# Sampled attention: scores in two products with the low rows added by VectorE, and part of the hi/lo splits moved to GpSimd

## The reference, cut to what matters

```python
def sample_attn(q, k, v, lam, k_past, v_past, rel_bias):
    s_past = diff_logits(q, q_pos, k_past, jnp.arange(past), rel_bias)
    s_new = diff_logits(q, q_pos, k, q_pos, rel_bias)
    w = diff_weights(jnp.concatenate([s_past, s_new], axis=-1), lam)   # softmax 0 - lam * softmax 1
    return (jnp.einsum('bhqk,bkhe->bqhe', w[..., :past], v_past)
            + jnp.einsum('bhqk,bkhe->bqhe', w[..., past:], v))
```

## Time and the profile before

| | |
|---|---|
| median of the runs | 2069.2 us |
| profiled execution | 2068.8 us, of which the span is 2066.9 us |
| TensorE matmul busy over the span | 2020.3 us (98%) |
| weight loads / VectorE / ScalarE / GpSimd busy | 1880.8 / 1386.9 / 991.8 / 12.4 us |
| sampled turns (first keys turned to last scores) | 843.5 to about 1073.6 us |
| output projection behind them | up to about 1206 us |

### The profile page before, as it was taken

One profiled execution on the slowest core, in us unless ns is written; L12 is line 12 of the kernel. 1 busy time (PEld: TensorE's weight loads), 2 busy tenths in 40 slices (PEclk: granted clock), 3 DMA queues, 4 the chain that ended last, 5 costly groups with the idle time before them and its releaser, 6 DMA issues. The chain is left out here.

```text
span 2066.9 us, 36364 instructions
## 1 busy us (share of the span) xinstructions
PE 2020.3 (98%) x12096; PEld 1880.8 (91%) x12096; DVE 1386.9 (67%) x3022; ACT 991.8 (48%) x1824; POOL 12.4 (1%) x42
## 2 busy tenths in 40 slices
PE   7999999999999999899999999999999999999998
PEld 6999999999999999888987899999999898989896
DVE  6766676767676766688885467575757574847476
ACT  5757575757575747677774333231313131413133
POOL 0000000000000000000000000000000000000000
PEclk9999999999999999999999999999999999999999
DMA  6411111112111112787782121111202020202012
GB/s 201 138 57 53 56 52 56 58 54 58 49 58 50 58 51 86 293 287 271 284 279 89 58 81 52 36 58 32 62 22 72 22 72 22 62 22 70 12 52 98
DMA packets 167421, 183.01 MB, mean 89 GB/s; under 512 B 11077, under 2 KB 139621, under 8 KB 167317
## 3 DMA queue, kind: packets, MB, share of 16 engines
q1 hardware_dynamic: 166105, 180.98, 27.0%
q10 hardware_dynamic: 1212, 0.81, 0.1%
HBM read 162.56 MB, written 24.46 MB: 90 GB/s over the span
## 5 line engine op out<-in xcount | busy, mean ns | idle before, releaser
L1247 PE MATMUL ps<-h_hi,w_hi 128*128 128x384 f32 (+1 forms) x1152 | 386.5, 336 | 10.2 <-DVE v_lo L1170 6.8
L1247 PE MATMUL ps<-h_hi,w_lo 128*128 128x384 f32 (+1 forms) x1152 | 376.6, 327 | 0.0
L1247 PE MATMUL ps<-h_lo,w_hi 128*128 128x384 f32 (+1 forms) x1152 | 376.4, 327 | 0.0
L2333 PE MATMUL ps<-h_hi,f_w_hi 128*128 128x320 f32 (+1 forms) x1136 | 370.7, 326 | 0.8 <-PEq L1532 0.8
L2333 PE MATMUL ps<-h_hi,f_w_lo 128*128 128x320 f32 (+1 forms) x1136 | 370.4, 326 | 0.0
L2333 PE MATMUL ps<-h_lo,f_w_hi 128*128 128x320 f32 (+1 forms) x1136 | 370.2, 326 | 0.0
L2412 ACT ACTIVATE yc<-ps,f_prm 128x384 f32<-128x384 f32 x144 | 93.5, 654 | 553.8 <-PE ps L2333 391.0
L2313 PE MATMUL ps<-d_hi,act 128*128 128x512 f32 x816 | 257.1, 390 | 1.6 <-DVE d_lo L2516 1.6
L1247 PEld LDWEIGHTS ps<-h_hi,w_hi 128*128 128x128 f32 x1152 | 217.4, 189 | 13.5 <-DVE v_lo L1170 7.2
L1247 PEld LDWEIGHTS ps<-h_lo,w_hi 128*128 128x128 f32 x1152 | 217.0, 188 | 0.6
L1247 PEld LDWEIGHTS ps<-h_hi,w_lo 128*128 128x128 f32 x1152 | 216.7, 188 | 0.0
(11 more groups left out here) (308 smaller groups left out, 3585.3 us busy)
## 6 DMA issues: line engine op xcount, KB each, us to landing
k<-in_cache_k SPq DMA_DIRECT2D x64, 512.0 KB, 5.9
v_raw<-in_cache_v SPq DMA_DIRECT2D x64, 512.0 KB, 4.6
w_raw<-in_w_in SPq DMA_DIRECT2D x48, 512.0 KB, 4.0
f_raw<-in_w_up SPq DMA_DIRECT2D x48, 512.0 KB, 4.0
f_raw<-in_w_down SPq DMA_DIRECT2D x24, 512.0 KB, 3.5
bias<-bias_tiles_dram SPq DMA_DIRECT2D x8, 576.0 KB, 3.7
merged_dram<-mg SPq DMA_DIRECT2D x8, 544.0 KB, 2.7
ow_raw<-in_w_out SPq DMA_DIRECT2D x8, 512.0 KB, 6.4
```

The costliest lines, as they stand in the source:

```text
L1247: last_ = pe.matmul(bank(s)[:, 0:n], w[:, W_SLOT[g], k, :], x[:, k, off:off + n], start=(k == 0 and i == 0), stop=(k == KT - 1 and i == 2))
L2333: l_ = pe.matmul(ps[:, e % 6, 0:n], w[:, p, k, :], x[:, k, off:off + n], start=(k == 0 and i == 0), stop=(k == KT - 1 and i == 2))
```

## The change

The query operand becomes one tile `qd`. For heads 0 to 3 its columns 0 to 63 hold the high parts and 64 to 127 the low parts; for heads 4 to 7 it is the other way round. Two products per chunk (by `kt_hi` and by `kt_lo`) then give the high rows and the low rows of four heads. After heads 0 to 3, and again after heads 4 to 7, ScalarE copies the 64 low rows out of PSUM to `slo` (`low_rows`), and VectorE adds them to the 64 high rows into `P` (`sum_rows`). TensorE's scores of head 4, and of the next turn's head 0, wait for that sum. Bias and maximum are then taken from `P` in SBUF.

The new keys and new values are split once for all sequences (`kn`, `vn`); GpSimd copies the 8 new keys of a head next to the turned ones (`new_key`) and lays the new weights into their own columns (`new_weights`), so that the new values take two matmuls of 128 rows. GpSimd also makes the low parts of value pages 1, 3, 5 and 7, and of output weight rows 0 to 3 in the last turn. The weights are turned before the scores of head 2 in place of after them. Page 2 is applied ahead of the scores of head 4, and later pages mostly one per head. In ScalarE's list `copy_o2` stands ahead of the exponential, and keys stand ahead of the split of the weights.

```diff
-SPLIT_AT = {2: (0,), 3: (1,), 4: (2, 3), 5: (4, 5), 6: (6,), 7: (7,)}
-PV_AT = {4: (0, 1), 5: (2, 3), 6: (4, 5), 7: (6, NPAGES), 8: ()}
+HH = H // 2
+SPLIT_AT = {2: (0, 1), 3: (2,), 4: (3,), 5: (4, 5), 6: (6,), 7: (7,)}
+PV_EARLY = {5: (2,)}
+PV_AT = {4: (0, 1), 5: (3,), 6: (4,), 7: (5,), 8: (6, NPAGES)}
...
+OUT_LOW = [x for x in OUT_SPLITS if x[0] == "m" or x[1] >= 4]
+POOL_LAST = [x for h in range(H + 1)
+             for x in [("v", n) for n in SPLIT_AT.get(h, ()) if n in POOL_PAGES]
+             + [x for x in OUT_AT.get(h, ()) if x not in OUT_LOW]]
...
+    def q_hi_of(part, m, h0):
+        return strips(part, 144 * h0 + DEC_T * m)
+    def q_lo_of(part, m, h0):
+        return strips(part, 144 * h0 + DEC_T * m + (NS if h0 < HH else -NS))
+    def half_rows(s):
+        lo = slice(NS, 128) if s == 0 else slice(0, NS)
+        hi = slice(0, NS) if s == 0 else slice(NS, 128)
+        return hi, lo
...
+            def new_key(b, h):
+                if at_start(b) and h == 0:
+                    pool.wait_ge(new_lo, 1)
+                if not (at_start(b) and h < 2):
+                    pool.wait_ge(qkh_done, 8 * b + h - 1)
+                    pool.sem_inc(settled, 1)
+                pool.tensor_copy(kt[:, :, h % 2, PAST:NKEYS], kn[:, :, h, bass.ds(DEC_T * b, DEC_T)])\
+                    .then_inc(ktn_done, 1)
+            def new_weights(b):
+                if has(b, 2):
+                    pool.wait_ge(pt_done, b - 1)
+                    pool.sem_inc(settled, 1)
+                    pool.tensor_copy(p_new[:, :, bass.ds(DEC_T * (b - 2), DEC_T)], zeros[:, :, :]).then_inc(s_fill, 1)
+                pool.wait_ge(exp_done, b)
+                pool.sem_inc(settled, 1)
+                pool.tensor_copy(p_new[:, :, bass.ds(DEC_T * (b - 1), DEC_T)], new_twice).then_inc(s_fill, 1)
+            def weights_low(h):
+                for what, k in OUT_AT.get(h, ()):
+                    if what == "w":
+                        pool.wait_ge(hi_done, OUT_SPLITS.index((what, k)) + 1)
+                        pool.tensor_tensor(w_rows(c.ow_lo, k), w_rows(c.ow_raw, k), w_rows(c.ow_hi, k).bitcast(F32),
+                                           ALU.subtract).then_inc(vplo_done, 1)
+            def body(b, u):
+                for h in range(H):
+                    if has(b, 0):
+                        new_key(b, h)
+                    if h == 2 and has(b, 1):
+                        new_weights(b)
+                    if has(b, 1):
+                        for n in splits_of(b).get(h, ()):
+                            if n in POOL_PAGES:
+                                pool.wait_ge(vhi_done, 8 * (b - 1) + n + 1)
+                                pool.tensor_tensor(v_lo[:, n, :], v_raw[:, n, :], v_hi[:, n, :].bitcast(F32),
+                                                   ALU.subtract).then_inc(vplo_done, 1)
+                    if isinstance(b, int) and b == LAST:
+                        weights_low(h)
+                if isinstance(b, int) and b == LAST:
+                    weights_low(H)
...
             def page(b, n):
-                k = 128 if n < NPAGES else DEC_T
-                pe.wait_ge(vnlo_done if n == NPAGES else vlo_done, b if n == NPAGES else 8 * (b - 1) + n + 1)
+                if n == NPAGES:
+                    pe.wait_ge(new_lo, 2)
+                elif n in POOL_PAGES:
+                    pe.wait_ge(vplo_done, pool_low(b, ("v", n)))
+                else:
+                    pe.wait_ge(vlo_done, len(DVE_PAGES) * (b - 1) + DVE_PAGES.index(n) + 1)
                 for hf in range(2):
                     cols = slice(512 * hf, 512 * (hf + 1))
-                    pair = (v_hi[:, n, cols], v_lo[:, n, cols]) if n < NPAGES else (vn_hi[:, cols], vn_lo[:, cols])
-                    for x, v in enumerate(pair):
-                        last = pe.matmul(o2[:, cols], pt_both[0:k, n, :, :].rearrange("p a n -> p (a n)"), v,
+                    parts = (v_hi[:, n, cols], v_lo[:, n, cols]) if n < NPAGES else (vn[:, cols],)
+                    for x, v in enumerate(parts):
+                        last = pe.matmul(o2[:, cols], pt_both[:, n, :, :].rearrange("p a n -> p (a n)"), v,
                                          start=(n == 0 and x == 0), stop=(n == NPAGES - 1 and x == 1))
...
+                        pe.matmul(ptn, p_new[:, :, :].rearrange("p x n -> p (x n)"), C[:, :], start=True, stop=True,
                                   skip_group_check=True).then_inc(pt_done, 1)
-                        if isinstance(b, int) and b == DEC_B:
-                            out_tile(1, range(0, 4))
+                    if has(b, 1):
+                        for n in PV_EARLY.get(h, ()):
+                            page(b, n)
+                    if h >= 1 and has(b, 0):
+                        g = h - 1
+                        if g == 0:
+                            if not at_start(b):
+                                pe.wait_ge(sum_done, 2 * b)
+                            pe.wait_ge(qdlo_done, 4 * b + 2)
+                        if g == HH:
+                            pe.wait_ge(sum_done, 2 * b + 1)
+                            pe.wait_ge(qdlo_done, 4 * b + 4)
+                        pe.wait_ge(ktlo_done, 16 * b + 2 * g + 2)
+                        pe.wait_ge(ktn_done, 8 * b + g + 1)
+                        for cc in range(3):
+                            keys = slice(SC * cc, SC * (cc + 1))
+                            for x, k in enumerate((kt_hi, kt_lo)):
+                                last = pe.matmul(S3[:, cc, :], qd[:, 128 * g:128 * (g + 1)], k[:, g % 2, keys],
+                                                 start=(g % HH == 0 and x == 0), stop=(g % HH == HH - 1 and x == 1))
+                        last.then_inc(qkh_done, 1)
+                    if h == 2 and has(b, 2):
+                        fold_heads(b - 1)
+                    if h == 3 and isinstance(b, int) and b == DEC_B:
+                        out_tile(1, range(0, 4))
                     if h >= 4 and has(b, 1):
                         if h == 4:
                             pe.wait_ge(ptlo_done, 2 * b)
...
+            def low_rows(b, s):
+                hi, lo = half_rows(s)
+                act.wait_ge(qkh_done, 8 * b + HH * (s + 1))
+                act.activation(slo[hi, :].rearrange("p (a n) -> p a n", a=3), S3[lo], ACT.Copy)\
...
                        .then_inc(kthi_done, 1)
-                act.activation(kt_hi[:, h % 2, PAST:NKEYS], c.k_new[:, h, bass.ds(DEC_T * b, DEC_T)],
-                               ACT.Copy).then_inc(ktn_hi, 1)
...
-                    if has(b, 0) and (h > 0 or at_start(b)):
-                        keys(b, h)
+                        act.activation(pt_hi[:, NPAGES, :], ptn, ACT.Copy).then_inc(pthi_done, 1)
                     if h == 0 and at_start(b):
-                        act.wait_ge(s_fill, 2)
...
-                    if h == H - 1 and has(b, 0) and has(b, -1):
-                        queries(b + 1, 0, H - 2)
+                        act.wait_ge(s_fill, 1)
+                        queries(0, 0)
+                        act.activation(kn[:, 0, :, :], c.k_new[:, :, :], ACT.Copy).then_inc(new_hi, 1)
+                        queries(0, HH)
+                    if h == 1 and has(b, 0) and has(b, 1):
+                        queries(b, HH)
+                    if h == HH and has(b, 0):
+                        low_rows(b, 0)
+                        if has(b, -1):
+                            queries(b + 1, 0)
+                    if h == HH + 1 and isinstance(b, int) and b == 1:
+                        act.wait_ge(vn_in, 32)
+                        act.activation(vn[:, :], vn_raw[:, :], ACT.Copy).then_inc(new_hi, 1)
+                    if h == 1 and has(b, 2):
+                        copy_o2(b - 1)
                     if h == 1 and has(b, 1):
                         act.wait_ge(nmx_done, b)
                         act.activation(P[:, :], P[:, :], ACT.Exp, bias=mx[:, 1:2], accum_out=mx[:, 2:3])\
                            .then_inc(exp_done, 1)
...
+            def sum_rows(b, s):
+                hi, _ = half_rows(s)
+                dve.wait_ge(slo_done, 2 * b + s + 1)
+                dve.tensor_tensor(P[hi, :].rearrange("p (a n) -> p a n", a=3), S3[hi],
+                                  slo[hi, :].rearrange("p (a n) -> p a n", a=3), ALU.add).then_inc(sum_done, 1)
...
                         dve.wait_ge(pthi_done, 2 * b)
                         dve.tensor_tensor(pt_lo[:, 0:NPAGES, :], pt.rearrange("p (n k) -> p n k", n=NPAGES),
                                           pt_hi[:, 0:NPAGES, :].bitcast(F32), ALU.subtract).then_inc(ptlo_done, 1)
-                        dve.tensor_tensor(pt_lo[0:DEC_T, NPAGES, :], ptn, pt_hi[0:DEC_T, NPAGES, :].bitcast(F32),
+                        dve.tensor_tensor(pt_lo[:, NPAGES, :], ptn, pt_hi[:, NPAGES, :].bitcast(F32),
                                           ALU.subtract).then_inc(ptlo_done, 1)
...
```

(50 more changed lines are left out.)

162 lines of the change are left out of this document (70 added, 92 removed).

## The result

The changed kernel takes 2058.33 us (median; 2057.56 to 2058.44) against 2069.22 for the kernel before on the same chip. The ratio is 0.9942, with an interval of 0.993 to 0.9955. The forecast was 2049.4, its range 2036 to 2062: faster, as forecast, but by 10.9 us and not by 19.4. The span of the profiled execution fell from 2066.9 to 2056.5 us.

A forecast was written before the change was run, and what follows sets the result against it. TensorE was taken as the bound, busy 229.2 of 230.1 us. Six turns' worth at 3.0 give 18.0; turn 0 -0.3, turn 1 +2.6, turn 7 -1.5, eighth body +0.6: 2068.8 - 19.4 = 2049.4 us, range 2036 to 2062.

The forecast's parts named there:

- T and S: TensorE's turning of one head's keys, 0.79 us, and one head's scores, 1.51 us before and 1.03 forecast.
- the forecast work of 25.4: TensorE's work in a full turn: 29.9 us less 3.84 for scores and 0.65 for new values.
- T2: Key turning after the hand-over: waits for `kt_lo` of head 1, which VectorE takes after the maximum; 0.7 us a turn.
- T3: Next key turning: waits for `kt_lo` 2, since ScalarE's exponential stands ahead of keys 2; 0.7 us a turn.
- Page 3: Value page behind low rows and queries in ScalarE's order, so GpSimd has it late: TensorE waits 0.4 us a turn.
- Loads are hidden: A turn's 8.5 MB takes 24.0 us at the first turn's 355 GB/s, under the turn's 27.3.
- The gain of 0.9 in the first scores: Turn 0: about 0.9 us won in its first scores, which ran at the lower clock level.
- GpSimd's queue (page 5, two rows, page 7 ...): Turn 7: operations from 18.6, each 2.3 us, give page 7 at 27.8, so the turn ends 1.5 us later.
- rival (2): VectorE and GpSimd hold each other up: 0.3 us a turn, 5 in turn 7; 2056 to 2062; chance 0.18 for 2055 to 2064.5.
- (1): All TensorE stalls hidden: the full 35.9 us less, 2032.9, or 2040 with one 0.7 stall a turn; chance 0.20.
- (3): Slower because GpSimd's subtraction is slow: gain gone at about 4 us each, 2090 at 4.8; chance 0.08.
- (4): Nothing changes: losses of (2) and some of (3) cancel the 19.4 us gain; chance 0.04.

The follow-up runs named there:

- the late maximum: Changed kernel with the maximum behind head 1's low keys, and exponential and scale behind head 2's keys: 2058.99 us, 0.9945.
- page 3 early: Changed kernel with value page 3 split at head 3 in place of head 4: 2054.05 us, 0.9923.
- The last experiment: The kernel with the other orders, with output tile `m0` split at head 4 in place of head 3 of turn 7: 2045.22 us, 0.9884.
- the kernel with the other orders: Changed kernel with page 3 split early, output rows on VectorE, new values loaded behind pages, maximum and exponential late except in the eighth body: 2048.39 us, 0.9891.

## Why the prediction came out as it did

**TensorE's work.** T and S have the forecast lengths (896.62 - 895.83 = 0.79, 900.44 - 899.42 = 1.02). Held against the 27.63 of turn 2, the forecast work of 25.4 leaves 2.2 us of holds; the prediction had 1.8 of them.

**The holds of a turn.** All three came where they were put, and were put down to the engines named. Before T2: TensorE was free at 896.62 + 1.03 = 897.65 and started at 898.41, 0.76, and 899.42 - 898.41 - 0.79 = 0.22 more between the halves; forecast 0.7 in all. Before T3: 900.44 + 0.87 = 901.31 against 901.65, 0.34, and 902.74 - 901.65 - 0.79 = 0.30 between the halves; forecast 0.7. Page 3: 0.7, forecast 0.4. The experiments hold them up one by one: the late maximum takes away 0.4 us of the first two (turns of 27.25 and 27.11 for 27.63 and 27.54), the early split takes the third, and both together give 26.4, still 1.0 over the work. So the order explains a part of the first two holds; what sets the rest was not tested. The forecast was 3.0 us a turn and the chip gave 2.77: over five turns 1.2 of the missing 9.0 us (19.4 less the 10.4 by which the spans differ).

**GpSimd.** Forecast 2.3 us, measured 2388 ns for the output rows and 2536 ns on the mean of the 32 pages, lengthened ones included. The Trainium skill's 2.25 ("GPSIMD Engine Reference", section "Elementwise — side-by-side cycle accounting", an estimate from its figure) is near too; the measurement decides, and neither moves the sum by more than 0.2 us a turn (page 3, for which TensorE waits, took 2.45).

**Turns 0 and 1.** Keys of head 1 of turn 2 start at 895.83, against 893.65 before. The forecast was 2.3 earlier, they came 2.2 later: 4.5 of the missing us. Of these, 0.6 is where the stage began (844.12 against 843.50), which says little: with nothing changed ahead of it, the other variants began between 843.30 and 845.17. The sums cost 1.24 and 1.25, less than the 1.76 forecast.

Three terms were missing or too large. The step "Loads are hidden" failed in turn 0: a wait of 1.36, which goes with the order of the new values' loads. The gain of 0.9 in the first scores didn't come: from the first keys to those of head 3 it took 6.23 us (844.12 to 850.35) against 6.37 (843.50 to 849.87), so 0.1 was won. The start ran at the lower of TensorE's two levels for longer: its first 3.88 us have a granted clock of 0.50, the kernel before had 0.58 over 4.00, and the lower stretch is about 6.8 against 3.4 us. That explains little of it, for page 3 early had 3.4 us again and still took 6.01 (843.76 to 849.77, with a wait of 0.36 in it). And in turn 1, with the new values' split ahead of pages 4 and 5 in ScalarE's list and of page 4 in VectorE's, GpSimd's page 5 took 3.12 us (885.34), the key copy behind it 1.33 for two, and TensorE waited 1.02. The load is shown by two experiments; the order in turn 1 is read from the timelines and was not tested by itself.

**Turn 7 and the end.** Up to the keys of head 1 of turn 7 the kernel was 11.6 us ahead of the one before, at the fold of the last sequence 10.4: 1.2 lost, where a gain of 3.0 - 1.5 + 0.6 = 2.1 was forecast, 3.3 of the missing us. The term that failed is "GpSimd's queue (page 5, two rows, page 7 ...)". It counts pages and rows and leaves out the new keys in the same queue, on which TensorE's scores wait, and it prices rows at 2.3 us with nothing for VectorE and GpSimd holding each other up. The new keys' place alone isn't the cause: put ahead of the rows, they left a wait of 2.13 us at the same scores, now for VectorE's `kt_lo`. The rows on VectorE took the wait from 3.08 to 1.20 and won 2.7 us of the stretch up to the last fold, and the pages on VectorE won 2.3, which shows that the cost is GpSimd's work in turn 7 beside VectorE's. Some 1.5 us of it is the lower level behind the gap, which the prediction named as a way to fail and put into no sum. How much is queue and how much is mutual hold was not separated. A further part is `m0`: in the changed kernel ScalarE waited 0.59 us for its load at 1044.00 and then split it, and TensorE waited 0.77 for the keys behind it. The last experiment shows that its place sets such a wait, in the kernel with the other orders (2.26 us, gone with the split one head later); in the changed kernel itself it was not tried.

1.2 + 4.5 + 3.3 = 9.0, which is all of it; the medians differ by 0.5 more than the two profiled spans. So the mechanism was right for the turns in the steady state, and what was put down for turn 0, turn 1 and turn 7 was too favourable. The point forecast and its own band (2044 to 2055, chance 0.50) were missed. That the time still lies inside 2036 to 2062 is owed to rival (2), whose band the range took in.

**The rivals.** (1), all holds hidden, didn't happen, and comes nearer with other orders: its turn of 25.4 became 26.37, with 1.0 us of holds left. (2), VectorE and GpSimd hold each other up, is right as a mechanism, and its time (2056 to 2062) was hit, in part by luck: half of what the prediction missed lies in turns 0 and 1, where (2) put nothing. The rule of the Trainium skill, "SBUF — State Buffer", section "Who interferes with whom", agrees with these runs: VectorE's subtraction of two SBUF operands took 3.18 and 2.88 us beside a GpSimd one, where it takes 1.22, and two of 32 elements took 2.05 for 0.39. But it cost next to nothing in the turns between 1 and 7: moving the pages off GpSimd left them at 27.57. It costs where GpSimd's queue is full or ScalarE feeds it early, so the price I put on it in each turn (0.3) was in the wrong place. That for turn 7 was in the right one, of 5 us on two waits: VectorE's page took 2.71 us, and the last maximum 3.41 for 1.23 (1066.16), which TensorE's output matmuls covered. (3), a slow GpSimd, is out at 2.4 us, and (4) with it. Of the named ways to fail, two happened: TensorE falls to its lower level behind the gap of 2.77 us in turn 7 (0.57 over the next 4 us), and VectorE operations next to GpSimd's were much longer than in the earlier trace rows.

## What to carry to other kernels

When work goes to an idle engine, write its whole queue down, the copies of 16 elements too, and who waits for each. Then look at what its large operations do to the engine that it relieves: here moving the small copies forward won 0.4 us, and taking the large ones away won 2 to 3. Turns in the steady state were forecast within 0.3 us from distances between starts; first and last turns need a list of their own, with the loads that others queue ahead of them. A long gap of TensorE is to be priced with the clock behind it. And a stall that is taken away pays only if the next one in the order isn't as late: here five small changes of order and place together gave 12 us, as much as the change itself, while the late maximum alone gave nothing.

## What the runs showed of the hardware

- An instruction of VectorE with both inputs in SBUF and one of GpSimd that reads SBUF are not worked on together. VectorE: 1.22 us becomes 1.52, 1.90, 2.71, 2.88 or 3.18 by how far GpSimd's 2.4 has got, and a maximum of 128x1032 3.41 where it takes 1.23; GpSimd: 2.39 becomes 3.12, and a copy of 16 elements 1.19 to 1.20 where it takes 0.20 alone. VectorE's subtractions with an input in PSUM keep their length (1.29 for two, beside GpSimd's page at 910.27).
- GpSimd's subtraction of 128x1024 takes 2.36 to 2.40 us undisturbed, twice VectorE's. The ones of 2.44 to 2.50 begin some 0.2 us before such an operation of VectorE ends.
- The clock fell behind a gap of TensorE in turn 7: granted 1.00 in the window with the gap and 0.57 in the one after; a matmul of 512 columns then starts 0.43 us behind the last one instead of 0.23 (1060.78, 1061.21). The holds of 0.5 to 0.9 us in every turn left it at 1.00. The length of a gap didn't decide it alone: with waits of 1.25 and 1.14 us at the head of turn 1 it stayed at 1.00 in the changed kernel (869 to 873) and fell with page 3 early (0.57 over 868 to 872).
